# Seams of a two-layer trunk kernel rebuilt: norms split, request groups interleaved, buffers moved

## The reference, cut to what matters

```
mod = silu(cond) @ w_mod + b_mod                 # 6 x D per group
sh1, sc1, g1, sh2, sc2, g2 = split(mod, 6)
h   = x * (1 + sc1) + sh1
x   = LN(alpha * x + g1 * Mixer(h)) * ln_g[0] + ln_b[0]
h   = x * (1 + sc2) + sh2
x   = LN(alpha * x + g2 * ffn(h))   * ln_g[1] + ln_b[1]
```

## Time and profile before

| | |
|---|---|
| median of 3 runs | 2048.93 us (2047.83 to 2052.78) |
| profiled execution | 2053.18 us, span from first to last instruction 2050.9 us |
| granted TensorE clock over the span | 0.966 |
| PE busy | 1901.2 us, 93% |
| DVE busy | 1461.4 us, 71% |
| ACT busy | 1143.0 us, 56% |
| chain that ended last | PE 88%, DVE 5%, ACT 3%, issue 2%, DMA 1% |
| moved | 529.61 MB, 258 GB/s over the span |

### The profile page before, as it was taken

The page is one execution under the profiler, slowest core; times in us unless marked ns, Lnnn a source line. Parts: engine busy times, 40 slices in busy tenths (PEclk is TensorE's granted clock), DMA queues, the critical chain, the costliest instruction groups (busy, mean ns, idle before and its releaser), DMA issues.

```text
span 2050.9 us, 25166 instructions
## 1 busy us (share of the span) xinstructions
PE 1901.2 (93%) x9102; PEld 1422.6 (69%) x9102; DVE 1461.4 (71%) x1795; ACT 1143.0 (56%) x1358; POOL 29.8 (1%) x53
## 2 busy tenths in 40 slices
PE   4999999789996999998699999999999999999994
PEld 1775464467884874553488888888888888888883
DVE  1447863434546448853598998989989899898995
ACT  2452232234433451331487887778878788787872
POOL 1000010000000000000000000000000000000000
PEclk8999999889997999999799999999999999999997
DMA  9555442546655645341599999999999999999990
GB/s 344 200 205 205 169 168 84 188 143 236 220 184 187 210 165 201 113 150 41 182 362 361 339 365 341 359 341 357 363 335 365 343 353 366 333 366 344 353 366 24
DMA packets 226992, 529.61 MB, mean 258 GB/s; under 512 B 4824, under 2 KB 7328, under 8 KB 226928
## 3 DMA queue, kind: packets, MB, share of 16 engines
q1 hardware_dynamic: 222848, 516.96, 69.9%
q0 software_dynamic: 3168, 9.80, 1.5%
q10 hardware_dynamic: 912, 1.97, 0.3%
HBM read 526.10 MB, written 2.62 MB: 258 GB/s over the span
## 4 chain that ended last, share of the span: by engine, by line
PE 88%; DVE 5%; ACT 3%; issue 2%; DMA 1%; ACTq 0%; DVEq 0%; POOL 0%; SPq 0%; POOLq 0%
PE ps L808 20%; PE ps L809 19%; PE ps L810 19%; PE ps L741 14%; PE ps L762 2%; PE ps L765 2%; PE ps L764 2%; PE ps L1142 2%; PE ps L775 2%; PE ps L798 1%; PE ps L1163 1%; DMA ring<-in_w_mod 1%; ACT arena L1255 1%; PE ps L1039 1%; ACT hT L1313 0%
## 5 line engine op out<-in xcount | busy, mean ns | idle before, releaser
L2097 DVE TENSOR_TENSOR arena_r<-ring,arena_r 128x1024 fp32r<-128x1024 f32 x448 | 539.9, 1223 | 38.2 <-ACT arena_r L1547 16.5
L1547 ACT ACTIVATE arena_r<-ring 128x1024 fp32r<-128x1024 f32 x448 | 474.1, 1061 | 118.9 <-PE ps L810 116.0
L808 PE MATMUL ps<-arena_r 128*128 128x512 f32 x1128 | 449.3, 398 | 22.5 <-DVE arena_r L1599 14.1
L809 PE MATMUL ps<-arena_r 128*128 128x512 f32 x1128 | 442.5, 392 | 0.0
L810 PE MATMUL ps<-arena_r 128*128 128x512 f32 x1128 | 413.2, 392 | 0.0
L2097 DVE TENSOR_TENSOR ring_r<-ring,ring_r 128x1024 fp32r<-128x1024 f32 x224 | 271.0, 1223 | 40.7 <-ACT ring_r L1547 37.7
L1547 ACT ACTIVATE ring_r<-ring 128x1024 fp32r<-128x1024 f32 x224 | 235.8, 1060 | 61.0 <-PE ps L810 59.6
L808 PEld LDWEIGHTS ps<-arena_r 128*128 128x128 f32 x1128 | 214.6, 190 | 68.1 <-issue 23.3
L808 PE MATMUL ps<-ring_r,arena_r 128*128 128x512 f32 (+1 forms) x592 | 239.4, 404 | 16.7 <-DVE ring_r L1599 8.3
L810 PEld LDWEIGHTS ps<-arena_r 128*128 128x128 f32 x1128 | 214.6, 190 | 46.9
L809 PEld LDWEIGHTS ps<-arena_r 128*128 128x128 f32 x1128 | 215.0, 191 | 44.3
(11 more groups left out here) (243 smaller groups left out, 1897.4 us busy)
## 6 DMA issues: line engine op xcount, KB each, us to landing
ring<-in_moe_w_gate SPq DMA_DIRECT2D x56, 2048.0 KB, 7.8
ring<-in_moe_w_up SPq DMA_DIRECT2D x56, 2048.0 KB, 8.0
ring<-in_moe_w_down SPq DMA_DIRECT2D x56, 2048.0 KB, 8.9
ring<-in_w_in SPq DMA_DIRECT2D x28, 2048.0 KB, 10.6
ring<-in_w_mod SPq DMA_DIRECT2D x24, 2048.0 KB, 9.0
ring<-in_ffd_w_gate SPq DMA_DIRECT2D x5, 2048.0 KB, 10.8
ring<-in_ffd_w_up SPq DMA_DIRECT2D x5, 2048.0 KB, 7.7
ring<-in_ffd_w_down SPq DMA_DIRECT2D x5, 2048.0 KB, 7.6
```

Source lines behind the costliest of these rows:

```text
L808: mm(o_, hi, w_hi[:, n], start=start, stop=False)
L809: mm(o_, hi, w_lo[:, n], start=False, stop=False)
L1547: act_(split_part(j)[0], raw_part(j), ACT.Copy).then_inc(part_hi, 1)
L2097: V.tensor_tensor(w_lo, raw_part(j), w_hi.bitcast(F32), ALU.subtract).then_inc(part_lo, 1)
```

## The change

Norms: `layer_norm` is split into `standardize` (mean, variance, subtract and scale; sets `x_ready`) and `affine` (gain, bias). For three of the four norms the gain and bias go into the scale and shift columns that the turned eviction applies (`mod_columns(..., fold)`: sh + sc * bias, sc * gain), with the columns of ln_g and ln_b loaded and turned once at the start. `affine` is done later on the tokens, as the residual needs it.

Order: the two groups are interleaved. In seams A and C, mod 11 stands ahead of the mix product, group 0's turn between the mix products of group 1, the gate rows inside the wait for group 1's norm, and in seam C the tokens of group 0 are turned before group 1's norm. The last four parts of the dense down product go group by group. In seam B the mod units 4, 5, 8, 9 are done, 8 and 9 of layer 1 no longer in mixer 1. `mod_turn` is cut from `mod_unit` and put behind other products.

Buffers: parts of the dense layer and the experts lie in the arena only; ring slot 3 holds the SiLU and activation buffers, the experts' sum and the last norm's gain and bias; the slot of a unit is that which is done with earliest, where before slots went round.

The diff, cut to its core:

```diff
@@ the list of products and units @@
     for l in range(DEPTH):
         if l:
             mod(l, 4)
-        for g in range(G):
-            p("hT", l, g, 0), p("hT", l, g, 1)
-            if l and g == 0:
-                mod(l, 5)
-            p("v", l, g)
+            p("hT", l, 0, 0), p("hT", l, 0, 1)
+            for i, after in ((4, 5), (5, 8), (8, 9)):
+                mod_turn(l, i), mod(l, after)
+            p("hT", l, 1, 0), p("hT", l, 1, 1)
+            mod_turn(l, 9)
+            p("v", l, 0), p("v", l, 1)
...
         mod(l, 10)
-        for g in range(G):
-            p("mT", l, g, 0), p("mT", l, g, 1)
-        for g in range(G):
-            p("mix", l, g, 0), p("mix", l, g, 1)
+        p("mT", l, 0, 0), p("mT", l, 0, 1)
+        mod_turn(l, 10)
+        mod(l, 11)
+        p("mT", l, 1, 0), p("mT", l, 1, 1)
+        mod_turn(l, 11)
+        p("mix", l, 0, 0), p("mix", l, 0, 1), p("mix", l, 1, 0)
+        p("h2T", l, 0, 0), p("h2T", l, 0, 1)
+        p("mix", l, 1, 1)
...
-    SLOT.append((_i - _first) % (XRING if ("wg", 0) in UNITS[:_i + 1] and ("v", 1) not in UNITS[:_i + 1] else RING))
+    SLOT.append(min(range(len(_held)), key=lambda _s: (done_with(UNITS[_held[_s]]) if _held[_s] >= 0 else -1, _held[_s], _s)))
@@ buffers @@
             if phase_of(j) == "dense":
-                return split_part(s)
+                b = (18432, 23040, 0, 2048)[s]
+                return arena_r[:, b:b + PART], arena_r[:, b + PART:b + 2 * PART]
...
             s = j % PARTS
-            b = ring_r[:, s * 2 * PART:(s + 1) * 2 * PART] if s < 2 else arena_r[:, (s - 2) * 2 * PART:(s - 1) * 2 * PART]
-            return b[:, 0:PART], b[:, PART:2 * PART]
+            b = s * 2 * PART if s < 4 else 10240 + (s - 4) * 2 * PART
+            return arena_r[:, b:b + PART], arena_r[:, b + PART:b + 2 * PART]
@@ SP @@
                 if name[0] not in ("mod", "wg", "wu", "wd") and name[-1] == 1 and SLOT[i] == RING - 1:
-                    await_product(sp, "Y", 1, 1)
+                    await_product(sp, "aT", len(FCHUNKS) - 1, 1)
@@ PE, dense down product @@
-                            for g in range(G):
-                                fs = slice(f * T + g * P, f * T + (g + 1) * P)
-                                inss = split_mm(...)
...
+                    for g in range(G):
+                        for f in range(FF_D // P - DPARTS, FF_D // P):
+                            inss = down_part(f, [g])
+                            if f == FF_D // P - 1:
+                                full(inss[0], "Y", g, 0), full(inss[1], "Y", g, 1)
@@ ACT, seam B @@
+                    norm_sqrt(1)
+                    await_product(sc, "Y", 1, 1)
+                    hi_part("v", 0)
+                    mod_rows(l, 4, mrow3)
+                    sc.wait_ge(mod_ready, 2 * l + 1)
+                    modulated("hT", 0, 8, 0)
+                    high_h("hT", l, 0)
+                    hi_part("v", 1)
+                    mod_columns(l, 4)
+                    mod_rows(l, 5, mrow3)
+                    mod_columns(l, 5)
+                    norm_sqrt(1)
+                    mod_rows(l, 8, mrow3)
+                    hi_part("v", 2), hi_part("v", 3)
+                    mod_columns(l, 8)
+                    mod_rows(l, 9, mrow3)
@@ DVE @@
-            def layer_norm(xg, gain, bias_, sig):
+            def standardize(xg, sig=None):
                 moments([xg[:, 0:512], xg[:, 512:1024]])
                 rstd(stat[:, 37:38], stat[:, 38:39])
-                st.done(V.tensor_scalar(xg, xg, stat[:, 36:37], stat[:, 38:39], ALU.subtract, ALU.mult))
+                st.done(V.tensor_scalar(xg, xg, stat[:, 36:37], stat[:, 38:39], ALU.subtract, ALU.mult), sig)
+
+            def affine(xg, gain, bias_, sig=None):
                 st.done(V.tensor_tensor(xg, xg, gain, ALU.mult))
                 st.done(V.tensor_tensor(xg, xg, bias_, ALU.add), sig)
...
+                    for n in range(2):
+                        residual(1, gbc2, ("Y", 0, n), 0, n)
+                    normed(0)
+                    lo_part(1, "v", 0)
+                    residual(1, gbc2, ("Y", 1, 0), 1, 0)
+                    modulated(1, "hT", 0, 8, 0)
+                    residual(1, gbc2, ("Y", 1, 1), 1, 1)
+                    low_h(hm_lo, 0)
+                    normed(1)
```

More of the change, by code:

```diff
@@ L120, in w_token, with mg @@
         u((name, l), (name, l, G - 1))
-    def mg(l, n):
-        p("mg", l, 0, n), p("mg", l, 1, n)
+    def mg(l, n, turn=None):
+        p("mg", l, 0, n)
+        if turn is not None:
+            mod_turn(l, turn)
+        p("mg", l, 1, n)
         u((MG[n], l), ("mg", l, 1, n))
     for i in EARLY:
-        mod(0, i)
+        mod(0, i), mod_turn(0, i)
+    p("lncols")
     for l in range(DEPTH):
@@ L223, in plan @@
         else:
-            for g in range(G):
-                p("htok", g, 0), p("htok", g, 1)
             p("logits",), p("rank",)
@@ L1051, in _ @@
                                                  for j in range(4)])
[L1052 to L1057 removed]
+                    mod_turn(l, 10 + g, mrow)
+                    if g == 0:
+                        mod_unit(l, 11, mrow)
@@ new lines, in gate_taken @@
+                def gate_taken(g):
+                    take(sil_d[:, g * 512:g * 512 + FCHUNKS[0][1]], ("G", 0, g), ACT.Silu)
+                if l == 0:
+                    for j in range(D0, D0 + 2):
+                        early_hi(j)
+                norm_sqrt(1)
+                sc.wait_ge(mod_ready, 2 * l + 2)
+                modulated("h2T", 24, 32, 0)
+                if l == 0:
+                    high_h("h2T", l, 0)
+                    for j in range(D0 + 2, D0 + DPARTS):
+                        early_hi(j)
+                    norm_sqrt(1)
+                    gate_taken(0)
+                    modulated("h2T", 24, 32, 1)
+                    high_h("h2T", l, 1)
+                    residual_gates()
+                    gate_taken(1)
```

439 lines of the change are left out of this document (279 added, 160 removed).

## The result

The changed kernel takes 1976.38 us (1974.45 to 1976.97) where the kernel before takes 2049.08 (2047.83 to 2052.78): a ratio of 0.9645, 95% interval 0.9632 to 0.9659, 72.7 us less. The forecast was 1989, 59.9 less, with 1971 to 2009 as its range and 1978 to 1999 as the likeliest case's own. So sign, size and range hold, and the time lies just under the likeliest case's range.

What follows compares the result with a forecast made beforehand. TensorE was taken as full in the experts, with 69 us idle in three seams. Terms 23.5 + 5.2 + 2.2 + 2.9 - 4 + 5.2 + 14.9 + 10.5 - 0.5 = 59.9 gave 1989 us, range 1971 to 2009.

Steps and rivals of the forecast that it cites:

- Experts and parts: Parts out of the ring save 6.6 ns per matmul, plus 4.4 us at switches: experts +10.5 us, dense +2.9.
- Rival 2: Experts and dense layer: the address brings nothing, cadence follows something accompanying it; 10.5 + 2.9 us less, 2002; chance 0.13.
- Rival 4: Experts become bound by transfers, late units make PE wait; at 0.5 us more per unit, 2073; chance 0.04.
- Seam C: Mixer 1 to experts: shorter norm wait, early diagonal, full-speed gate rows, half the token turns gone: +14.9 us (10 to 16).
- Dense layer: Dense layer: +2.2 us from modulation turns no longer waiting for ACT's copy, +2.9 (0 to 3) from parts in the arena.
- Seam A: Mixer 0 to dense layer: interleaved groups remove waits and slow matmuls before the second gate chunk: +23.5 us (17 to 26).
- Mixer 0: Mixer 0: six waits for copies of modulation rows, 6.1 us, go; DVE's 4.8 wait limits it: +5.2 us (3 to 6.1).
- Mixer 1: Mixer 1: mods 8 and 9 and turn waits go, PE 8 us earlier; DVE follows by 4.84: +5.2 us (3 to 8).
- Seam B: Dense to mixer 1: v's load comes late, engines stand; T is the down product's end: -4 us (-8 to +13).
- Rival 1: Seam B: v isn't late, or engines don't stand behind it; ends near T+31, 17 us earlier, 1972; chance 0.10.
- Rival 3: Seams give half, each wait replaced by the next on DVE: A and C 19 us instead of 38.4, 2008; chance 0.14.
- Rival 5: Whole change: it doesn't do what it says, waits keep turns and norms in place; about 2030; chance 0.02.

Runs made afterwards that it cites:

- experiment 5: Changed kernel with two of the experts' six part places put back into the ring's last slot: 1987.1 us, experts' loop 1002.6 us.
- experiments 5 and 7: The second: changed kernel with two part places back in the ring's last slot and the ring allocated above the arena: 1977.2 us, loop 991.3 us.
- experiment 6: Changed kernel with the arena allocated ahead of the ring, lowest in the memory: 1977.5 us, experts' loop 991.3 us.
- experiment 10: Changed kernel with group 0's turn behind the whole mix product in seams A and C, as before: 1989.35 us, ratio 0.9714 to the kernel before.
- experiment 9: Changed kernel with gain and bias applied in the norm again instead of folded into the scale and shift columns: 1989.3 us, ratio 0.9716 to the kernel before.
- experiment 11: Changed kernel with mixer 0's modulation turns (units 4 to 9) right behind their products again: 1984.6 us, ratio 0.9697 to the kernel before.
- Experiments 2 and 3: Changed kernel with mod units 8 and 9 of layer 1 back in mixer 1: alone 1960.3 us; with v's load also moved first, 1960.5 us.
- experiment 1: Changed kernel with layer 1's v load moved ahead of mod units 4, 5, 8, 9 in the load list: 1962.5 us, ratio 0.9581 to the kernel before.
- experiment 4: Changed kernel with v's load first, mod units 8 and 9 in mixer 1, and group 1's norm ahead in VectorE's queue: 1960.75 us, ratio 0.9569.

## Why the prediction was right, point by point

**Experts and parts (10.5 and 2.9 forecast, 10.8 measured for the experts).** Right in size, and shown for the experts: experiment 5 gives back 10.7. The count of rows times 6.6 ns held, with part of the 4.4 for the matmuls behind a switch. So did the choice to trust the row against the rule of the Trainium skill that it was weighed with ("SBUF — State Buffer", section "SBUF: two separate sides"). The rule speaks of contention; these runs don't show one, but they don't exclude one either. What they show is that the amount of transfers isn't it: the same weights go through the loop in experiments 5 and 7, at a DMA share of 0.95 and 0.97, and the matmuls on the same ring slot are slow in 5 alone. Rival 2's price fell, but a part of its wording holds: "by the address" is not shown, since experiment 6 has a part at 49,152 at the full cadence, and something that goes with the address in the layout of before is the cause. Rival 4 fell as well: at 349 GB/s the loop is PE busy for 992.23 of 992.25.

**Seam C (14.9 forecast, 15.0 measured)** came out as worked out, in this profile; where it is 71.2 us long the gain is 13.4. The gate rows are at 3.60 there, as the text asked. The place of group 0's turn carries 5.6 of the gain (experiment 10) and the fold up to 3.9 (experiment 9); the rest is not tested by itself. **Dense layer (5.1 forecast, 5.7 measured):** PE's idle time there went from 2.15 us (177.00 less 174.85 busy) to none (171.80 of 171.80), which is the 2.2 for the turns. The other 3.5 stand where 2.9 were forecast for the parts; no experiment puts the parts of the dense layer back.

**Seam A (23.5 forecast, 28.9 measured).** The order of events was right, the term under-sized by 5.4. Counted from the mix's first matmul, group 1's gate product starts at 41.2 us where the text had 43.2, and the up product ends at 60.8 where it had 64.5: 2.0 from the chain of norm and split, and 1.7 in the up product, which the text had partly at the lower level. The 1.0 taken off for slow matmuls is the third piece. None ran slow in this profile, nor in nine of the experiments' in which seam A is as changed: it takes 70.9 us in all ten. In experiment 11, which doesn't edit seam A either, the up product is slow for 3 us behind the same wait, so the allowance was not absurd, but in ten of eleven profiles it was not needed.

**Mixer 0 (5.2 forecast, 10.1 measured).** 2.7 of the 10.1 lie ahead of mod 4's product, where no product was moved: 66.9 us from v's first product to it before, 64.2 after, 66.0 to 66.8 in the twelve experiments. The start ahead of it differs the other way, 47.0 after and 43.7 to 46.0 in the experiments. Counted from the start of the span, mod 4's product begins at 114.05 before and at 109.8 to 112.4 in all thirteen profiles since. There is one profile of before, and its execution was 4.1 us over the median, so whether these 2 to 4 us are the change's or that execution's is open. From mod 4 to mod 10 it is 7.4, and experiment 11 finds 5.9 of it. The other 1.5 are in the profile of before: behind the first of the six waits, 2.18 us, a turn took 1.11 and the matmuls came 0.43 us apart, where in experiment 11 the same wait is followed by a turn of 0.66 and matmuls 0.22 apart. What was wrong is the reason for the cap. VectorE's idle time ahead of the states fell, but it was not used up; before, then after:

```profile
211.17 0.29 DVE L1791 COPY arena<-ps 128x128 f32<-128x128 f32 x1 [4.83 <-PE ps L919]
...
200.42 0.29 DVE L1963 COPY arena<-ps 128x128 f32<-128x128 f32 x1 [1.62 <-PE ps L990]
```

PE's wait for DVE further on is 0.7 us in both profiles, so DVE's chain came forward by as much as PE did, and the 4.84 in the earlier trace rows was no bound for it. 6.1 uncapped would have been the better term.

**Mixer 1 (5.2 forecast, 6.0 measured).** The sum was right and one of its parts was not. DVE did become the later one, as forecast: new waits of PE for it,

```profile
791.07 0.66 PE L828 MATMUL ps<-cst,arena 128*128 128x128 f32 x4 [1.05 <-DVE arena L1918]
...
799.99 0.46 PE L1004 MATMUL ps<-arena,A 128*128 128x128 f32 x2 [1.70 <-DVE arena L1967]
```

but I credited this to mods 8 and 9 as well as to the turns. Experiments 2 and 3, with the units back and their turns apart, keep the gain but for 1.0: 262.8 us. With the units in, DVE still idles 1.62 us ahead of the states and PE waits 0.7 us for it, at a granted clock of 1.00 over the mixer; without them DVE's idle time is gone, PE waits 1.05 and 1.70, and the clock is 0.99. So taking the units out gave DVE the last 1.6 us that it could come forward by, and PE lost as much again. That the turns' waits are what the 6.0 come from is argued: no experiment puts them back in mixer 1.

**Seam B (-4 forecast, +2.6 measured; seam B and mixer 1 together 8.6, forecast 1.2).** The mechanism was right up to v's start: v fifth in SP's queue, issued at T+2.6 (measured 2.6, with T at 574.1), landing at T+16.6 (measured 15.7), ACT, DVE and PE behind it, v's product at T+32 to 35 (measured 30.5, a little early). The step that failed is the last: "its 24 matmuls, mostly at the lower level, and group 1's end at T+46 to T+50". The mods and turns ahead kept PE going, v's 48 matmuls ran 0.23 apart from the second on, and the end was at T+41.5. From v's start to the end that is 11.0 us where the text had 14 to 15, 3 to 4 of the 6.6; the rest is v's earlier start. Nor was it luck: the seam takes 41.2 to 41.4 us in six profiles in which it wasn't edited, and 42.9 in that of experiment 11. Rival 1 was near in its price, 17 us forecast against 13.9 measured (experiment 1), but as a forecast of the changed kernel it fell: the load was late. What I didn't see is the other half of the price: the two units that made it late bought nothing in mixer 1.

**Rival 3** (half of seams A and C) fell: 43.9 us came, where its 19 and the forecast's 38.4 were set. **Rival 5** fell with the order seen in the trace.

**The sum.** It was 59.9 where the profiles differ by 78.3 and the medians by 72.7. Every larger miss is to the same side: seam B 6.6, seam A 5.4, mixer 0 4.9. In the first two, 3 to 4 and 2.7 us are allowances for matmuls at the lower level that were hardly ever needed. In the third, 2.7 lie where nothing was moved, 1.5 in slow matmuls of the profile of before, and the rest in a bound that wasn't one. The 5.6 by which the profiles differ more than the medians are the two executions' own.

## What to carry to other kernels

Moving work into a seam moves its transfers ahead of everything that stands behind it in an in-order queue: ask of each move which load it now delays, and which engine's queue has an instruction on that load ahead of other work. Before moving work out of a stage, see in the trace which engine bounds that stage; here a stage in which VectorE could come forward by only 1.6 us more gave nothing that shows for TensorE work taken out of it. And where two places of an operand show two cadences in one stretch, count the matmuls and believe the row.

## What the runs showed of the hardware that was not expected

A matmul of 512 columns came 234 ns behind the one before where its moving operand lay in bytes 49,152 to 65,535 of a partition, with the token halves in the arena above it, and 227 ns in every other layout that was tried, among them one with a part on the first half of the same bytes, inside the arena (experiment 6). The first six matmuls behind such a part were slow in part, too (231 on average), though their own operands lay in the arena. It cost 10.7 us of 1987 (experiment 5). The same weights go through the loop in every layout, so the amount of transfers isn't the cause; what is was not found.

The same wait of 2.98 us ahead of the same product was followed by matmuls at the higher level in eleven profiles (0.23 us apart, as at 389.62 above) and by a dozen or more at the lower one in two (0.43 apart, experiments 9 and 11), 3 us apart in the end. In mixer 0 a wait of 2.18 us did the same (before, and experiment 11). And two shorter waits can lose part of what they gain: in experiment 4 waits of 1.94 and 2.11 us in place of one of 5.73 put v's start 2.4 us earlier, its first nine matmuls came 0.43 us apart, and seam B ended 1.1 us sooner.
